# Inverse roots in the attentions of a three-block transformer kernel: from Sqrt and reciprocal to Ln, Exp and a Newton step, with table loads placed by hand

## The reference

```python
def rms_norm(x, g):
    y = xf * lax.rsqrt(jnp.mean(xf * xf, axis=-1, keepdims=True) + EPS)
    return (y * g).astype(x.dtype)

# differential attention (layer 1): a norm over the 128 elements of each head's output
o = rms_norm(o, subln) * (1.0 - lam_init)

# forgetting attention (block 3): q and k of each of 8 heads are normed over 64 elements
t = t.reshape(B, S, N_HEADS, HEAD_DIM)
t = rmsnorm(t, g)
log_f = jax.nn.log_sigmoid(f_logit + b_forget)
```

## Time and profile before

| what | value |
|---|---|
| time, median of 3 runs | 2087.43 us (2087.04 to 2091.03) |
| span of the profiled execution | 2087.8 us |
| TensorE busy | 2043.2 us (98%), weight loads 1684.1 us (81%) |
| VectorE busy | 1224.2 us (59%) |
| ScalarE busy | 941.6 us (45%) |
| GpSimd busy | 904.8 us (43%) |
| mean granted TensorE clock | 0.992 |

### The profile page before, as it was taken

One profiled execution on the slowest core, in us unless ns is written; L12 is line 12 of the kernel. 1 busy time (PEld: TensorE's weight loads), 2 busy tenths in 40 slices (PEclk: granted clock), 3 DMA queues, 4 the chain that ended last, 5 costly groups with the idle time before them and its releaser, 6 DMA issues.

```text
span 2087.8 us, 28730 instructions
## 1 busy us (share of the span) xinstructions
PE 2043.2 (98%) x9976; PEld 1684.1 (81%) x9976; DVE 1224.2 (59%) x1842; ACT 941.6 (45%) x1495; POOL 904.8 (43%) x660
## 2 busy tenths in 40 slices
PE   7999999999999999899999999999999999999999
PEld 6777788888887878788888887878888788888887
DVE  6677857546265789856636266548879473213222
ACT  5456645434245567635424245535742544322222
POOL 4322235545456431044645456444215454455454
PEclk9999999999999999999999999999999999999999
DMA  4222122332323211022333223222103222232323
GB/s 169 81 76 76 48 75 98 103 101 91 101 91 121 81 61 32 31 91 81 101 101 101 92 99 112 91 81 92 39 23 107 85 91 92 90 110 92 101 91 111
DMA packets 52756, 183.21 MB, mean 88 GB/s; under 512 B 6576, under 2 KB 6832, under 8 KB 52656
## 3 DMA queue, kind: packets, MB, share of 16 engines
q1 hardware_dynamic: 51072, 177.76, 25.9%
q10 hardware_dynamic: 1584, 4.07, 0.5%
HBM read 176.04 MB, written 2.10 MB: 85 GB/s over the span
## 4 chain that ended last, share of the span: by engine, by line
PE 53%; issue 24%; POOL 13%; DVE 7%; ACT 2%; POOLq 0%; DVEq 0%; DMA 0%; ACTq 0%; SPq 0%
PE PS L544 52%; POOL wlo L536 13%; DVE AR L1915 1%; PE PS L773 1%; DVE AR L1918 0%; DVE acc L1630 0%; DVE ptlo L1805 0%; DVE AR L1797 0%; DVE nmax L1753 0%; ACT AR L1187 0%; DVE AR L2277 0%; ACT AR L1323 0%; DVE AR L1931 0%; DVE Blo L1935 0%; DVE Blo L2281 0%
## 5 line engine op out<-in xcount | busy, mean ns | idle before, releaser
L536 POOL TENSOR_TENSOR wlo<-raw,whi 128x512 fp32r<-128x512 f32 x656 | 904.6, 1402 | 1169.7 <-ACT whi L1090 1168.5
L544 PE MATMUL PS<-Bhi,whi 128*128 128x512 f32 x2352 | 927.7, 394 | 17.2 <-DVE Blo L1623 10.8
L544 PE MATMUL PS<-Blo,whi 128*128 128x512 f32 x2352 | 917.6, 390 | 0.0
L544 PE MATMUL PS<-Bhi,wlo 128*128 128x512 f32 x2352 | 917.4, 390 | 0.0
L1090 ACT ACTIVATE whi<-raw 128x1024 fp32r<-128x1024 f32 x328 | 345.2, 1056 | 510.7 <-PE PS L544 435.4
L544 PEld LDWEIGHTS PS<-Bhi,whi 128*128 128x128 f32 x2352 | 442.5, 188 | 123.1 <-issue 14.1
L544 PEld LDWEIGHTS PS<-Bhi,wlo 128*128 128x128 f32 x2352 | 442.6, 188 | 93.7
L544 PEld LDWEIGHTS PS<-Blo,whi 128*128 128x128 f32 x2352 | 443.0, 188 | 89.3 <-issue 0.5
L1614 DVE TENSOR_TENSOR AR<-PS,R 128x512 f32<-128x512 f32 x170 | 115.3, 690 | 235.9 <-PE PS L544 224.1
L1670 DVE TENSOR_TENSOR X<-X,PS 128x512 f32<-128x512 f32 x88 | 60.3, 687 | 227.2 <-PE PS L544 226.5
L1915 DVE SCALAR_TENSOR_TENSOR AR<-AR,par_sb 128x511 f32<-128x511 f32 x88 | 117.6, 1336 | 8.8 <-ACT AR L1323 8.8
(11 more groups left out here) (237 smaller groups left out, 2069.1 us busy)
## 6 DMA issues: line engine op xcount, KB each, us to landing
raw<-in_weights SPq DMA_DIRECT2D x328, 512.0 KB, 3.2
AR<-AR SPq DMA_DIRECT2D x56, 64.0 KB, 2.0
X<-in_xT ACTq DMA_DIRECT2D x4, 512.0 KB, 6.9
out<-X SPq DMA_DIRECT2D x8, 256.0 KB, 3.0
AR<-in_pT ACTq DMA_DIRECT2D x2, 512.0 KB, 3.9
par_sb<-in_parameters ACTq DMA_DIRECT2D x1, 314.0 KB, 8.5
AR<-in_positions ACTq DMA_DIRECT2D x1, 256.0 KB, 8.3
con_sb<-in_constants ACTq DMA_DIRECT2D x1, 198.5 KB, 8.1
```

Of the source, the lines that this page charges most:

```text
L536: ins = pool.tensor_tensor(wlo[:, j, c], raw[:, j % RAWS, c], f32(whi[:, j, c]), ALU.subtract)
L544: return pe.matmul(out, w, x, start=start, stop=stop)
```

## The change

Within the first and the third attention an inverse root is no longer Sqrt on ACT and a reciprocal on DVE. ACT computes the logarithm and the exponential of minus half of it (for the head tiles after an extra Identity that brings the mean plus eps from PSUM to SBUF), and DVE improves the result y by one Newton step y(1.5 - 0.5 x y y), three instructions (`refined`) in place of the reciprocal. Ln and Exp are in one table, which is loaded by hand ahead of both attentions (`logs_and_exps`). The Sqrt table of `root` is loaded by hand ahead of the wait for the sums, a load of the Exp table follows the root of attn1, and a small Sqrt behind the first attention (it only loaded a table) is gone.

```diff
--- before.py
+++ after.py
@@ -228,6 +228,9 @@
         rcol = sb("rcol", [P, TB])
         rootc = sb("rootc", [P, TB])
         hinv = sb("hinv", [P, 2, 2 * TB])
+        hvar = sb("hvar", [P, 2, 2 * TB])
+        oroot = sb("oroot", [P, 32])
+        term = sb("term", [P, 32])
         mixc = sb("mixc", [P, 2 * TB])
         lam = sb("lam", [P, 8])
         gs = sb("gs", [P, 4])
@@ -442,6 +445,10 @@
             return epsq[:, 4 * BATCHES[b][0]:4 * BATCHES[b][1]]
+        def rooted(b):
+
+            return oroot[:, 4 * BATCHES[b][0]:4 * BATCHES[b][1]]
+
         def spread_bank(h):
             return 6 if h < 6 else 4 + h % 2
@@ -1084,6 +1091,10 @@
         def _(act):
             own = Own(act, act_step)
+            def logs_and_exps():
+
+                act.preload_act_table_set("natural_log_exp_and_others")
+
             def high(s, slot, half):
                 act.wait_ge(raw_ready[slot % RAWS], 16 * half + 16)
@@ -1123,6 +1134,7 @@
             def root(norm):
                 n = NORMS.index(norm)
+                act.preload_act_table_set("sqrt_and_others")
                 act.wait_ge(ss_done, n + 1)
                 act.activation(rootc[:, :], PS[:, 7, 0:TB], ACT.Sqrt, scale=1.0 / D, bias=eps[:, 0:1])\
                    .then_inc(root_ready, 1)
@@ -1245,7 +1257,9 @@
             def output_root(b):
                 act.wait_ge(ovar_ready, b + 1)
-                act.activation(columns(b), columns(b), ACT.Sqrt).then_inc(oroot_ready, 1)
+                own.step(act.activation(rooted(b), columns(b), ACT.Ln))
+                own.wait()
+                act.activation(rooted(b), rooted(b), ACT.Exp, scale=-0.5).then_inc(oroot_ready, 1)
             def normed_high(h):
@@ -1417,6 +1431,7 @@
             act.activation(sinT[:, :], angs[:, 1, :], ACT.Sin).then_inc(trig_ready, 1)
             act.activation(cosT[:, :], angs[:, 2, :], ACT.Sin).then_inc(trig_ready, 1)
+            logs_and_exps()
             act.activation(lam[:, 2:4], lam[:, 0:2], ACT.Exp).then_inc(trig_ready, 1)
             values("v1", (0,), 4, T)
             replaced("v1", 3)
@@ -1428,7 +1443,6 @@
             attention(1)
             output_square(7)
-            act.activation(nmax[:, 4:5], eps[:, 0:1], ACT.Sqrt)
             used("o1a", 0, 2)
             output_root(2)
             for h in (6, 7):
@@ -1446,6 +1460,7 @@
             embedding(0, "attn1")
             root("attn1")
+            act.preload_act_table_set("exp_and_others")
             for t in range(2):
                 swap_halves("kq2a", t, QT0[2] + t)
             for t in range(2):
@@ -1509,8 +1525,13 @@
                 if t >= 2:
                     act.wait_ge(hspread, t - 1)
-                act.activation(hinv[:, t % 2, :], PS[:, bank, 0:2 * TB], ACT.Sqrt, scale=1.0 / 64,
-                               bias=eps[:, 0:1]).then_inc(hroot_ready, 1)
+                own.step(act.activation(hvar[:, t % 2, :], PS[:, bank, 0:2 * TB], ACT.Identity,
+                                        scale=1.0 / 64, bias=eps[:, 0:1]))
+                own.wait()
+                own.step(act.activation(hinv[:, t % 2, :], hvar[:, t % 2, :], ACT.Ln))
+                own.wait()
+                act.activation(hinv[:, t % 2, :], hinv[:, t % 2, :], ACT.Exp, scale=-0.5)\
+                   .then_inc(hroot_ready, 1)
             def head_high(t):
                 _, b, u = place_of(3, t)
@@ -1651,6 +1672,16 @@
                 dve.tensor_copy(R[:, :], PS[:, 7, :]).then_inc(r_ready, 1)
                 dve.wait_ge(r_ready, n + 1)
+            def refined(out, x, y):
+
+
+                v = term[:, 0:y.shape[1]]
+                own.step(stt(v, y, -0.5, y, ALU.mult, ALU.mult))
+                own.wait()
+                own.step(tt(v, v, x, ALU.mult))
+                own.wait()
+                return stt(out, v, 1.5, y, ALU.add, ALU.mult)
+
             def rounds(n, per, body):
                 if n <= 2:
                     for i in range(n):
@@ -1818,7 +1849,7 @@
             def invert_output_root(b):
                 dve.wait_ge(oroot_ready, b + 1)
-                dve.reciprocal(columns(b), columns(b)).then_inc(orinv_ready, 1)
+                refined(columns(b), columns(b), rooted(b)).then_inc(orinv_ready, 1)
             def output_variance(b):
@@ -2204,7 +2235,8 @@
             def head_inverse(t):
                 dve.wait_ge(hroot_ready, t + 1)
-                dve.reciprocal(hinv[:, t % 2, :], hinv[:, t % 2, :]).then_inc(hinv_ready, 1)
+                y = hinv[:, t % 2, :]
+                refined(y, hvar[:, t % 2, :], y).then_inc(hinv_ready, 1)
             def head_norm(t):
                 bank, _ = tile_of(*qk3(t))
```

## The result

| | kernel before | changed kernel |
|---|---|---|
| median, 22 runs each | 2087.54 us (2084.37 to 2093.67) | 2091.05 us (2087.19 to 2097.01) |
| ratio | | 1.0015, 95% interval 1.0009 to 1.0022 |
| profiled execution, span | 2087.8 us | 2093.3 us |
| mean granted clock, profiled execution | 0.992 | 0.989 |

The change costs 3.1 us (0.0015 x 2087.5; 1.9 to 4.6). The sign was right and so were most of the places, the size was forecast too large (5.9 us). The median of 2091.05 us is also just under the 2091.6 us at which the forecast's "slower" began, so what came is its case "within", which had a chance of 0.38, and not "slower", which had 0.52.

The account below looks back on a forecast made before the run. TensorE, busy 2043.2 of 2087.8 us, was taken to bound the kernel. Terms -1.0 + 1.35 + 0.85 + 0.5 + 2.66 + 1.6 - 0.42 + 0.36 = +5.9 us on 2087.4 gave 2093.3 us, range 2086.0 to 2095.8.

Parts of the forecast that it names:

- Start: First root: its table load, moved ahead of the wait, starts VectorE's chain of angles 1.28 us earlier; -1.0 us.
- Step 18: First attention's output root: GpSimd starts earlier, VectorE's new instructions wait for it, and TensorE runs late; +1.35 us.
- Second attention: Ahead of it, the Exp load delays the swap_halves copies and so the value rows to TensorE; +0.85 us.
- Tiles 0 and 1: Third attention's first head tiles: VectorE meets GpSimd at tile 1 and is still behind when making tile 2; +0.5 us.
- Tile 2: Third attention's head tile 2: VectorE's first two instructions wait for GpSimd's two halves, delaying TensorE's spread; +2.66 us.
- The clock: Behind head tile 2: after standing 3.4 us, TensorE runs for a while at 1.2 GHz; +1.6 us.
- Step 2: Third attention: TensorE, now late, no longer waits for head_norm; -0.42 us.
- Tile 7 and the steps: Third attention: at tile 7 three instructions cost VectorE 0.36 more, freed exponentials wait for maxima instead; +0.36 us.
- Rival (a): VectorE's three instructions slip through without waiting for GpSimd: +0.6 us, 2088.0 us; chance 0.22.
- (b): Everything as forecast, but the clock does not drop at head tile 2: 2091.7 us; chance 0.16.
- (d): Every table load taken away was on the path: 17 loads, 22 us, giving 2066 us; chance 0.02.
- Rival (c): ScalarE's freedom shrinks waits behind the lower-clock stretch from 1519 to 1532: 5 us come back, 2088.3 us; chance 0.16.

Follow-up runs that it names:

- start_only: Kernel before with one edit: the first root's Sqrt table loaded ahead of its wait; ratio 0.9995 (0.9986 to 1.0004) to the kernel before.
- three_reciprocals: Changed kernel with ScalarE's exponential at plus 0.5 and three VectorE reciprocals instead of the Newton step; ratio 0.9998 (0.9987 to 1.0008) to the kernel before.
- direct: Changed kernel without Newton step, Identity and attn1's Exp load; one reciprocal, root ahead of slab copy at head tile 2; 0.9981 of the kernel before, repeated 0.9983.
- after_again: Changed kernel measured a second time, nothing edited; ratio 1.0018 (1.0007 to 1.0030) to the kernel before.
- output_only: Kernel before with only the first attention's part of the change; ratio 0.9996 (0.9987 to 1.0005) to the kernel before.

## Why the prediction was right, and where it was off

**Start, -1.0 forecast, -1.45 measured.** VectorE's chain passed the whole 1.25 us on to the value rows; the guess that GpSimd's slab would eat some of it was wrong. That the lower clock behind the stop might go was not priced; it did go, and was worth 0.2 us net, for the reason told under start_only. A stretch at the lower clock that goes without being named is one of the forecast's own signs of being wrong, and this one appeared. The measured value lies outside the term's bounds (0.8 and 1.3).

**Step 18, +1.35 forecast, +1.07 and +1.01 measured.** The meeting came as told: GpSimd's slab 1 us earlier in its step, VectorE's three at 0.83, 1.20 and 0.17 us. The term is too large by 0.3 us at the end of the chain: counted in the time of the kernel before, the second of the three ends at 193.0 and the third at 193.2, where the forecast had 193.1 and 193.5. Another sentence of the term is wrong, that the load taken from ahead of the exponentials "gives nothing here, since TensorE did not wait for them". In the kernel before the maxima are ready at 192.22, and the load holds the first exponential until 192.76:

```profile
191.00 1.22 DVE L1756 TENSOR_REDUCE nmax<-PS 128x1 f32<-128x512 f32 x2
191.47 1.28 ACT L1207 ACT_TABLE_LOAD   x1
192.76 0.69 ACT L1207 ACTIVATE AR<-PS,nmax 128x512 f32<-128x512 f32 x1
```

In three_reciprocals and direct, where the meeting is away, the step gains 0.5 us. The load had cost TensorE gaps too short to stand in the list of waits; their sum shows only when matmul is held against matmul.

**Second attention, +0.85 forecast, +0.79 and +0.63 measured.** 0.73 us, the direct path alone, would have been the better value. The rule of the Trainium skill ("ScalarE: Activation LUTs", "What ACT_TABLE_LOAD costs"), by which a drain of 1.38 us would have made it 2.2, is not borne out: the copy behind this load starts 0.01 us after its end.

```profile
725.34 1.28 ACT L1463 ACT_TABLE_LOAD   x1
726.63 4.81 ACT L1199 ACTIVATE AR<-PS 32x512 f32<-32x512 f32 x8
```

**Tiles 0 and 1, +0.5 forecast, 0.0 measured.** VectorE did meet GpSimd at tile 1 and lost more than a microsecond (1.25 us for 128x8):

```profile
1433.40 1.25 DVE L1679 SCALAR_TENSOR_TENSOR term<-hinv 128x8 f32<-128x8 f32 x1
```

But the difference of TensorE's starts changes by less than 0.01 us from 1418 to 1443 us. The backlog was real, 1.9 us behind the root of tile 1. Then VectorE's next group (`taps`, six instructions) took 4.06 us where it had taken 4.98, since GpSimd's slab was over, and 0.9 us of the backlog was left. TensorE did not feel these: up to the stop at tile 2 the difference of the starts stays as it is. The lower bound of the term, 0, was the right value.

**Tile 2, +2.66 forecast, +2.40 and +2.39 measured,** a wait of 3.11 us where 3.4 was forecast, against 0.72 before. Of all the terms this one decided the sign. **The clock, +1.6 forecast, +1.91 and +0.95 measured** (+2.34 and +0.98 in the other two kernels that have the stop). It drops each time, as forecast; the price hangs on whether the stretch is 3.4 or 6.8 us long. By half of these it would be 1.7 or 3.4 us. Less was measured: in the changed kernel 1.3 us of the stretch fall into the stop, and that the rest is absorbed by TensorE's short waits behind it is argued, not shown.

**Step 2, -0.42 forecast, -0.47 measured. Tile 7 and the steps, +0.36 forecast, -0.02 in both measured:** the wait for `hinv` at tile 7 grew as forecast, from 0.94 to 1.31 us. But the steps ahead of it gain 0.1 us, and TensorE's next wait falls from 2.35 to 2.08 us. So ScalarE's freedom, which the forecast took to be lost in waits for the maxima, gives back what VectorE's longer root costs; direct, with a short root, gains 0.44 to 0.55 there.

**The sum:** 5.9 forecast; 4.2 and 3.0 by the places, 3.1 and 3.8 (0.0018 x 2088.6) by the medians. The mechanism was right, but seven of the eight terms were set too high, by up to 0.5 us each, and only the clock erred in both directions (0.3 too low in one execution, 0.65 too high in the other). Rival (a), no meetings, is refuted by the durations at step 18 and tile 2, though at tile 1 the meeting cost TensorE nothing, as (a) had it; (b), no drop of the clock, by four executions; (d) by the time; (e), tables reloaded, by the list of loads (45 in all, 62 before). Rival (c) is half true. The stretch from 1519 to 1532 did not go by the change: it is 10.2 us long in the profiled execution of either kernel, 3.4 us in after_again, and also 3.4 us in start_only and output_only, which leave the third attention as it was. But a part of ScalarE's freedom is worth time, 2 us in direct, and the forecast gave it none.

**What stays open:** the precision that the Newton step adds was not measured. Why the lower clock behind tile 2 begins earlier in some executions, and lasts longer there, isn't shown.

## What to carry to other kernels

A VectorE instruction on a few elements is only cheap if its inputs don't meet GpSimd's: with two SBUF inputs it costs up to the rest of GpSimd's instruction, whatever its size (1.25 us at most here, for 0.17 alone), so a reciprocal replaced by three such steps has to be looked at against GpSimd's timetable. Before adding arithmetic to save table loads, ask which of the loads TensorE feels; here about 2 us of 22, and only where nothing else is late next. When two kernels run the same matmuls in the same order, subtract their starts: this showed terms of 0.5 us that the time, good to 2 us, could not.

## What the runs showed of the hardware

The profiled executions of the changed kernel and of after_again, the same instructions, end 5.4 us apart (their last matmuls at +5.49 and +0.07 against that of before). 1.2 us of it lie in the places above, 2.4 between 866 and 897 us, 2.5 between 1519 and 1539, 1.0 between 199 and 741, and -1.4 ahead of 47 us (the rest, -0.3 us, elsewhere). Behind 866 and 1519 us the time at 1.2 GHz comes in other lengths from one execution to the next (between 1510 and 1540 us it is 3.4, 6.8 or 10.2 us in all). The kernel before's own profile holds such an accident, which the reading ahead of the prediction did not tell apart from the code: VectorE waits for a small transfer, and TensorE behind it. None of the other eleven has such a wait of VectorE of over 0.6 us between 121 and 166 us.

```profile
142.32 0.69 DVE L1737 TENSOR_TENSOR AR<-PS,AR 128x512 f32<-128x512 f32 x1 [2.43 <-DMA AR<-AR]
```

```profile
144.40 0.39 PE L544 MATMUL PS<-pthi,Bhi 128*128 128x256 f32 x1 [0.95 <-DVE ptlo L1805]
```

In these eleven TensorE is 1.6 to 2.6 us quicker between 121 and 166 us. One profile gives the durations of instructions to a hundredth; of a stall behind a transfer it gives one sample.
